# Three-pass products for gate, up and down of every expert, with a ring of four high-part buffers

## The reference, cut to what matters

```python
x = x + y                                                   # mixer's result
x = x + hier_moe(rmsnorm(x, norm_ffn[i]), w_router..., w_gate[i], w_up[i], w_down[i])

def hier_moe(h, ...):      # top 1 of 4 groups, top 2 of 4 experts in it
    hid = silu(t @ w1[e]) * (t @ w3[e]); hid = hid * gate   # w1, w3: 1024 x 512
    y = hid @ w2[e]                                         # w2: 512 x 1024
```

## Time and profile before

| | us |
|---|---|
| median of 3 runs (lowest, highest) | 1147.72 (1146.89, 1152.04) |
| span of the profiled execution | 1150.0 |
| TensorE matmul busy | 1021.1 (89%) |
| DVE busy | 621.7 (54%) |
| ACT busy | 407.2 (35%) |
| POOL busy | 135.4 (12%) |
| moved by DMA | 286.62 MB, 249 GB/s over the span |

### The profile page before, as it was taken

One profiled execution on the slowest core, in us unless ns is written; L12 is line 12 of the kernel. 1 busy time (PEld: TensorE's weight loads), 2 busy tenths in 40 slices (PEclk: granted clock), 3 DMA queues, 4 the chain that ended last, 5 costly groups with the idle time before them and its releaser, 6 DMA issues.

```text
span 1150.0 us, 13292 instructions
## 1 busy us (share of the span) xinstructions
PE 1021.1 (89%) x5002; PEld 737.4 (64%) x5002; DVE 621.7 (54%) x793; ACT 407.2 (35%) x589; POOL 135.4 (12%) x143
## 2 busy tenths in 40 slices
PE   5999997699999999997299979959999999999950
PEld 4999885356666565664199978734665656666530
DVE  5377513566565565654722384255656666565617
ACT  6225312243433434333442452214333343433403
POOL 2201200010101000010610030010010000101024
PEclk8999998799999999999599989978999999999985
DMA  8920404759999999996714031159599999999924
GB/s 249 389 75 1 167 38 166 256 181 381 355 374 361 368 350 347 378 357 251 265 49 146 17 141 49 55 175 336 201 338 372 369 358 374 353 374 350 344 84 176
DMA packets 118683, 286.62 MB, mean 249 GB/s; under 512 B 8554, under 2 KB 10090, under 8 KB 118636
## 3 DMA queue, kind: packets, MB, share of 16 engines
q1 hardware_dynamic: 104815, 236.27, 57.6%
q0 software_dynamic: 13584, 49.14, 11.4%
q10 hardware_dynamic: 244, 0.65, 0.2%
HBM read 258.06 MB, written 28.23 MB: 249 GB/s over the span
## 4 chain that ended last, share of the span: by engine, by line
PE 71%; DMA 13%; DVE 7%; issue 4%; ACT 3%; POOL 1%; SPq 1%; POOLq 0%; ACTq 0%; DVEq 0%
PE ps L621 42%; PE ps L716 14%; DMA wbuf_up<-in_w_up 10%; PE ps L724 7%; DVE x L1381 2%; PE ps L708 2%; ACT arena_c_r L1051 2%; PE ps L686 2%; PE ps L769 1%; DMA arena_a<-yrows,slots 1%; PE ps L596 1%; POOL arena_a L573 1%; DMA arena_a<-xrows,ids 1%; PE ps L740 1%; DVE arena_c L1558 1%
## 5 line engine op out<-in xcount | busy, mean ns | idle before, releaser
L716 PE MATMUL ps<-wbuf_gate,arena_a 128*128 128x512 f32 x512 | 230.5, 604 | 5.5 <-DVE arena_a L1221 5.5
L716 PEld LDWEIGHTS ps<-wbuf_gate,arena_a 128*128 128x128 f32 x512 | 98.6, 193 | 119.5 <-issue 110.6
L621 PE MATMUL ps<-wbuf_gate_r,wbuf_up_r 128*128 128x256 f32 (+1 forms) x768 | 169.5, 287 | 2.4 <-DVE wbuf_gate_r L1416 2.4
L1416 DVE TENSOR_TENSOR wbuf_down_r<-wbuf_down,arena_c_r 128x4096 fp32r<-128x4096 f32 x30 | 132.8, 4425 | 35.3 <-ACT arena_c_r L1051 35.3
L621 PE MATMUL ps<-arena_b_r,wbuf_up_r 128*128 128x264 f32 (+1 forms) x512 | 146.0, 285 | 0.0
L621 PEld LDWEIGHTS ps<-wbuf_gate_r,wbuf_up_r 128*128 128x128 f32 x768 | 129.3, 190 | 3.0 <-issue 2.7
L724 PE MATMUL ps<-wbuf_up,arena_a 128*128 128x512 f32 x256 | 117.6, 602 | 0.0
L1036 ACT ACTIVATE arena_a<-ps,vecT 128x128 f32<-128x128 f32 x128 | 36.6, 369 | 215.3 <-PE ps L708 215.3
L530 POOL DMA_INDIRECT arena_a<-xrows,ids x34 | 34.9, 1026 | 658.3 <-DVE ids L1213 657.7
L1051 ACT CAST arena_c_r<-wbuf_down 128x4096 fp32r<-128x4096 f32 x30 | 108.3, 3611 | 0.0
L1416 DVE TENSOR_TENSOR wbuf_up_r<-wbuf_up,arena_a_r 128x2048 fp32r<-128x2048 f32 x32 | 73.3, 2292 | 61.7 <-ACT arena_a_r L1058 60.1
(11 more groups left out here) (232 smaller groups left out, 1463.8 us busy)
## 6 DMA issues: line engine op xcount, KB each, us to landing
wbuf_up<-in_w_up SPq DMA_DIRECT2D x32, 2048.0 KB, 20.0
wbuf_gate<-in_w_gate SPq DMA_DIRECT2D x32, 2048.0 KB, 15.1
wbuf_down<-in_w_down SPq DMA_DIRECT2D x32, 2048.0 KB, 11.3
yrows<-arena_b POOLq DMA_DIRECT2D x32, 512.0 KB, 9.2
wbuf_gate<-in_w_in_even SPq DMA_DIRECT2D x2, 2048.0 KB, 11.0
wbuf_up<-in_w_in_even SPq DMA_DIRECT2D x2, 2048.0 KB, 9.2
wbuf_down<-in_w_out_even SPq DMA_DIRECT2D x2, 2048.0 KB, 26.2
yrows<-arena_c POOLq DMA_DIRECT2D x8, 512.0 KB, 12.3
```

Source lines behind the costliest of these rows:

```text
L621: last = pe.matmul(out, stationary[a](k), moving[b](k), start=(opens and i == 0), stop=(i == len(terms) - 1))
L716: last = pe.matmul(ps[:, 0, :], xgT[:, k, :], w[:, k, :], start=(k == 0), stop=(k == KC - 1))
L1416: dve.tensor_tensor(value_r, value, hi.bitcast(F32), ALU.subtract).then_inc(done, 1)
```

## The change

The gate and the up product become split products like the down product, and so does the last block's down product. Each matrix is handled in two groups of 2048 elements a partition. The high parts no longer have buffers of their own: four buffers of one group (`ring`) serve gate, up and down in turn, and a high part may be written when the product that used the slot last has finished its group; so `h1_mm`, `h3_mm` and `y_mm` now count groups, two a block. The low parts are still written over the loaded weights.

In body b, ACT now does: high part of group 0 of down(b-1), silu, high part of the hidden rows of b-1, group 1 of down(b-1), both groups of gate(b+1), high part of the rows of b+1 (1024 a partition out of PSUM), group 0 of up(b+1), the whole result of b-1 (1024), group 1 of up(b+1). DVE does the matching low parts, with the row numbers and the one-hot ahead of `hid`; it no longer copies results. The gate product of b waits for `xT_lo`, the low part of its rows, and for its first low group.

The norm's weight is multiplied in when the rows are scaled (`scale_rows`, odd phases), from a tile `g_ffn` that POOL loads once a layer. The final norm's weight moves to another place in SBUF.

The core of the diff:

```diff
-        up_hi = arena_a_r[:, 4608:4608 + UP_SPLIT * DE]
-        down_hi = arena_c_r[:, 0:4096]
+        ring = [arena_c_r[:, 0:GROUP], arena_c_r[:, GROUP:2 * GROUP],
+                arena_a_r[:, 6144:6144 + GROUP], arena_b_r[:, 2048:2048 + GROUP]]
...
+        def ring_slot(kind, par, g):
+            return ring[(g if par == 1 else 2 + g) if kind == GATE else
+                        (2 + g if par == 1 else g) if kind == UP else
+                        (g if par == 1 else 2 + g)]
+
+        def group_of(buf, g):
+            return buf[:, g * GROUP:(g + 1) * GROUP]
...
-                            sp.wait_ge(m[used], b - 1)
+                            sp.wait_ge(m[used], 2 * b - 2)
...
+                pool.dma_start(g_ffn, norm_ffn[l].partition_broadcast(P)).then_inc(ld_gffn, 16)
...
-                def gate(b, par, i):
-                    pe.wait_ge(ld_w[l][0][par], 16 * (before_same(b, par, i) + 1))
-                    w = as_kn(wbuf[0][par], KC)
-                    for k in range(KC):
-                        last = pe.matmul(ps[:, 0, :], xgT[:, k, :], w[:, k, :],
-                                         start=(k == 0), stop=(k == KC - 1))
-                    last.then_inc(m["h1_mm"], 1)
...
+                def first_product(kind, b, par, done):
+
+                    lo = m["gate_lo" if kind == GATE else "up_lo"]
+                    for g in range(2):
+                        pe.wait_ge(lo, 2 * b + g + 1)
+                        parts = [v.rearrange("p (c n) -> p c n", c=4)
+                                 for v in (ring_slot(kind, par, g), group_of(wbuf_r[kind][par], g))]
+                        split_product(ps[:, kind, :],
+                                      (lambda k: xT_parts[0][:, k, :], lambda k: xT_parts[1][:, k, :]),
+                                      (lambda k: parts[0][:, k - 4 * g, :], lambda k: parts[1][:, k - 4 * g, :]),
+                                      range(4 * g, 4 * g + 4), opens=(g == 0), closes=(g == 1)).then_inc(done, 1)
...
-                    pe.wait_ge(m["xT_d"], b + 1)
-                    pe.wait_ge(m["xT_a"], b + 1)
+                    pe.wait_ge(m["xT_lo"], b + 1)
...
-                down_last(2 * pairs - 1, pairs)
+                down(2 * pairs - 1, 1)
...
                 def rows_T(b):
                     need(act, m["xT_mm"], b + 1)
...
+                    act.copy(xT_flat[0], bank2(5)).then_inc(m["xT_hi"], 1)
...
+                def hi_gate(b, par, n, g):
+                    act.wait_ge(ld_w[l][GATE][par], 16 * n)
+                    need(act, m["h3_mm"], 2 * b - 1 + g)
+                    act.copy(ring_slot(GATE, par, g), group_of(wbuf[GATE][par], g)).then_inc(m["gate_hi"], 1)
+
+                def hi_up(b, par, n, g):
+                    act.wait_ge(ld_w[l][UP][par], 16 * n)
+                    need(act, m["y_mm"], 2 * b - 3 + g)
+                    act.copy(ring_slot(UP, par, g), group_of(wbuf[UP][par], g)).then_inc(m["up_hi"], 1)
+
+                def hi_down(b, par, n, g):
+                    act.wait_ge(ld_w[l][DOWN][par], 16 * n)
+                    act.wait_ge(m["h1_mm"], 2 * b + 3 + g)
+                    act.copy(ring_slot(DOWN, 1 - par, g), group_of(wbuf[DOWN][par], g)).then_inc(m["down_hi"], 1)
...
                 def body(b, par, i, last):
-                    hi_up(b, par, i)
...
+                    first = isinstance(b, int) and b == 0
+                    n = half_up(b, i)
+                    if not first:
+                        hi_down(b - 1, 1 - par, n, 0)
+                    act.wait_ge(m["h1_mm"], 2 * b + 2)
 
                     need(act, m["hid"], b)
                     act.activation(act_g, ps[:, 0, :], ACT.Silu).then_inc(m["silu"], 1)
+                    if not first:
+                        hidden_hi(b - 1)
+                        hi_down(b - 1, 1 - par, n, 1)
                     if not last:
...
+                        hi_gate(b + 1, 1 - par, n + 1, 0)
+                        hi_gate(b + 1, 1 - par, n + 1, 1)
                         rows_T(b + 1)
...
+                        hi_up(b + 1, 1 - par, n + 1, 0)
+                    if not first:
                         result(b - 1, 1 - par, (b - 1) // 2 if isinstance(b, int) else i - 1)
+                    if not last:
+                        hi_up(b + 1, 1 - par, n + 1, 1)
 
                 pairs = run_blocks(act, l, body)
+                for g in range(2):
+                    hi_down_last(2 * pairs - 1, g)
+                hidden_hi(2 * pairs - 1)
...
+                dve.scalar_tensor_tensor(out=xs[r, j, :],
+                                         in0=x[r, j, :],
+                                         scalar=rs[r, ph, j:j + 1],
+                                         in1=g_ffn[r, :],
+                                         op0=ALU.mult, op1=ALU.mult).then_inc(xs_done, 1)
...
+                dve.wait_ge(m["xT_hi"], b + 1)
+                low(xT_flat[1], bank2(5), xT_flat[0], m["xT_lo"])
...
                 def body(b, par, i, last):
                     first = isinstance(b, int) and b == 0
...
                     if not first:
...
+                        lo_group(DOWN, b - 1, 1 - par, 0)
+                        hidden_lo(b - 1)
+                        lo_group(DOWN, b - 1, 1 - par, 1)
+                    if not last:
+                        token_numbers(l, b + 2, par)
...
                     if not last:
+                        lo_group(GATE, b + 1, 1 - par, 0)
                         rows_T(l, b + 1)
...
+                        lo_group(GATE, b + 1, 1 - par, 1)
+                        lo_group(UP, b + 1, 1 - par, 0)
+                        lo_group(UP, b + 1, 1 - par, 1)
+
+                for g in range(2):
+                    lo_group(GATE, 0, 0, g)
+                for g in range(2):
+                    lo_group(UP, 0, 0, g)
                 pairs = run_blocks(dve, l, body)
```

More of the change, by code:

```diff
@@ L50 @@
 EPS = 1e-6
-UP_SPLIT = 4
+GROUP = 4 * DE
+GATE, UP, DOWN = range(3)
 MAX_OVER = 8
@@ L134, in trunk @@
         g_sgu = per_layer[:, 0:D]
+        g_ffn = per_layer[:, 0:D]
         eps = sb("eps", [P, 1])
@@ L613, in normed_tile, with split_product @@
                 transpose_tile(ph, j, (xs, x)[ph % 2][:, j, :], 4 + 2 * (j % 2)).then_inc(tr_done, 1)
-            def split_product(out, stationary, moving, chunks=range(KC), before=None, opens=True):
+            def split_product(out, stationary, moving, chunks=range(KC), before=None, opens=True, closes=True):
                 terms = [(k, a, b) for k in chunks for a, b in ((0, 0), (0, 1), (1, 0))]
@@ L735, in hidden_T, with gate, up @@
+                def gate(b, par):
+                    first_product(GATE, b, par, m["h1_mm"])
+                def up(b, par):
+                    first_product(UP, b, par, m["h3_mm"])
                 def hidden_T(b):
                     need(pe, m["hid"], b + 1)
-                    need(pe, m["hT_e"], b)
+                    need(pe, m["hT_lo"], b)
                     for c in range(FC):
@@ L743, in down @@
                 def down(b, par):
[L744 to L771, removed]
+                    need(pe, m["hT_lo"], b + 1)
@@ new lines, in down @@
+                    need(pe, m["y_out"], b)
+                    for g in range(2):
+                        need(pe, m["down_lo"], 2 * b + g + 1)
+                        parts = [v.rearrange("p (c n) -> p c n", c=2)
+                                 for v in (ring_slot(DOWN, 1 - par, g), group_of(wbuf_r[DOWN][par], g))]
+                        for k in (2 * g, 2 * g + 1):
+                            for h in range(2):
+                                cols = slice(h * 512, (h + 1) * 512)
+                                last = split_product(
+                                    ps[:, 2 + h, :],
+                                    (lambda k: hidT_parts[0][:, k, :], lambda k: hidT_parts[1][:, k, :]),
+                                    (lambda k: parts[0][:, k - 2 * g, cols], lambda k: parts[1][:, k - 2 * g, cols]),
+                                    range(k, k + 1), opens=(k == 0), closes=(k == FC - 1))
+                        last.then_inc(m["y_mm"], 1)
@@ L1030, in experts_blocks, with hidden_hi @@
                 m = moe[l]
-                row = 2 + l
                 def rows_T(b):
                     need(act, m["xT_mm"], b + 1)
-                    for c in range(4, KC):
-                        last = act.activation(xgT[:, c, :], ps[:, 6, (c - 4) * P:(c - 3) * P], ACT.Copy,
-                                              scale=vecT[:, c, row:row + 1])
-                    last.then_inc(m["xT_a"], 1)
+                    act.copy(xT_flat[0], bank2(5)).then_inc(m["xT_hi"], 1)
+                def hidden_hi(b):
+                    act.wait_ge(m["hT_mm"], b + 1)
+                    need(act, m["y_mm"], 2 * b)
+                    act.copy(hidT_flat[0], ps[:, 4, :]).then_inc(m["hT_hi"], 1)
@@ L1360, in body @@
                     if not last:
```

(19 more changed lines are left out.)

126 lines of the change are left out of this document (48 added, 78 removed).

## The result

The changed kernel takes 1195.88 us (median of 4 runs, 1191.13 to 1200.62), the kernel before beside it 1149.88. The ratio is 1.040, with a 95% interval of 1.036 to 1.043: 46 us slower, where I forecast 27. The direction was right; 1195.9 lies above the range of 1158 to 1193.

A forecast was written before the change was run, and what follows sets the result against it. TensorE was taken to bound the kernel, with DMA nearly as full. Start, bodies and end of the expert stretches gave +13.9 and +13.15 us, together +27.05 on 1150.0: 1177.1, less 2.3 for the median: 1174.8; range 1158 to 1193.

The forecast's parts named there:

- TensorE's work: Expert bodies: gate and up in three passes cut a body's work from 20.05 to 17.7 us.
- the new loop: Expert stretches: load and split before a gate product make two periods 40.7 us, one 20.35.
- E(b): End of the down product in body b, that of block b-1; the loads are issued after it.
- S(b): Start of body b's gate product; E(b) was forecast at 17.7 us after it.
- rival 3: Expert bodies: the clock falls in the idle gaps, 1 us a body, 1201, or 1188 in half of them; chance 0.16.
- S(2) to S(15): Steady part of each expert stretch, between these gate starts: +4.25 us in the first layer, +3.5 in the second.
- S(0) to S(1): First body of each expert stretch, first to second gate start: 17.9 us against 18.8, -0.9.
- S(1) to S(2): Second body of each expert stretch: 17.7 us for 20.35, -2.65.
- start and end: Each expert stretch: first gate 7.2 us later; from the last body's end to the result out, +8.0 us.
- nothing outside the stretches: Rest of the kernel outside the expert stretches: booked at 0 us.
- the norm: Row scaling with the weight: 1.7 us, some 0.9 more, ten times, hidden under other products, so 0.
- Rival 1: Expert stretches: loads come earlier and TensorE stays the bound, 1106 us; chance 0.06.

The follow-up runs named there:

- a_sp_order: The changed kernel with SP issuing each down load behind the next block's gate and up loads instead of ahead of them: 1115.09 us, ratio 0.971 to the kernel before.
- a_warm: The changed kernel with 32 extra products of 128 columns, work for nothing, behind each down product to fill the gap: 1185.38 us, ratio 1.031 to the kernel before.
- c_start: `a_sp_order` with DVE making block 0's two low gate groups ahead of the rest of `route`: 1105.09 us, ratio 0.960 to the kernel before.
- c_tail: `a_sp_order` with ACT making the last block's high down groups ahead of the result of the block before: 1100.60 us, ratio 0.955 to the kernel before.
- a_rows_first: The changed kernel with ACT copying the next rows ahead of both high gate groups, DVE following: 1168.62 us, ratio 1.017 to the kernel before.

## Why the prediction was right and wrong

**Right: TensorE's work.** Passes of 0.228 us, 17.7 us forecast for a body, 17.88 in `a_sp_order`. The gain of 2.2 us a body is real, and the changed kernel didn't collect it.

**Right: the new loop.** It runs from E(b) over load and split to the gate two bodies on; the order of the loads and the length of the way were each tested alone, with 81 and 27 us. Its cycle was forecast at 40.7 us and is 40.9 to 41.2 in the first layer, but this agreement is luck in part: two of its terms are off and nearly cancel. From S(b) to E(b) the body behind the gap takes 19.8 us and not 17.7, and the gate's load lands 15.2 us after E(b) (1.3 and 13.9) and not 16.8. The way behind it is 6.2 us, as forecast.

**Wrong in its step: every body after the first at full clock.** The sum has "TensorE idles 2.6 us a body" and then 17.7 us of work; the half clock behind the idling was left to rival 3 and stands in the sum with nothing. Since the loop spans two bodies, two interleaved chains run side by side, and only one of them waits: 3.5 us, then none. The prediction shared the wait out evenly without a reason. Behind each of the 14 longer gaps the gate ran in part at half clock. That was dear where no load's landing gives the time back: in the second body, in the last one and in the products of the mixer (below). In the loop most of it was absorbed, by what `a_warm` shows: from S(2) to S(15) the forecast is missed by only 1.6 us in the first layer and 4.8 in the second, of 22 in all.

The period of over 20 us had also seemed to be borne out by DMA, a batch needing 20.0 us from first byte to last landing. That was a time with queueing in it: at 17.88 us a body, in `a_sp_order`, the same bytes fit.

Rival 3, which I gave 0.16, named the mechanism, and its price (1188 to 1201) held the result. The price is luck in part too: its 26 us were to come from the loop, which came out 6.4 us over the forecast in both layers together. Its argument against, dense work on both sides, does not protect. The rule quoted there from the Trainium skill, TensorE: Matmul & The Clock Gate, section "HAM oscillation", fits: the clock was lower after each of these waits for a load. What stayed open in the trace of before (a 2.2 us wait to a fall, at the earlier trace rows) should have weighed more than the density.

**Mis-sized by the same cause.** S(0) to S(1) and S(1) to S(2) came out 0.5 to 2.3 us worse than forecast and the last body up to 3.1 (its gate 8.61 us at clock 0.84): in each a gate ran in part at half clock behind a gap (8.5 us for the first gate where I had 7.8; 7.35 for the second, behind a gap of 3.3 us that my own sum contains and doesn't price). Together with the last bodies this is 10.5 of the 22 us.

**Right: start and end.** +7.2 and +8.0 against +7.3 and +8.0, +7.3; `c_start` and `c_tail` name the queue order behind each.

**Wrong: nothing outside the stretches.** Of the 4.3 us between them about 3 are TensorE's: the first product of the second layer's mixer takes 4.60 us for 3.47, the products behind the mixing 23.76 for 22.43, and the mixing and the router 0.7 us more. Another 1.0 us is in two gathers (6.03 for 5.72 us, 5.67 for 4.97). Windows of the changed kernel have 0.77 there, the kernel before 1.00 at the same place:

```profile
717.00:724.00 7.00, 7.00 (x25) 5.70 (x26) 4.34 (x7) 2.78 (x4) 0.00 (x0) 0.77 0.23 82
```

```profile
693.40:700.00 6.60, 6.60 (x29) 5.36 (x30) 4.19 (x7) 2.79 (x4) 0.00 (x0) 1.00 0.24 84
```

Code and work are the same there. In `a_sp_order` the products behind the mixing take 22.43 again, but the first product 4.47. That the place of the clock's fall relative to the work decides is argued, not shown; no run was made for it, and one profile of each kernel can't tell it from chance. Why the gathers took longer stays open.

**Right with a wrong size: the norm.** 0 us; the scaling costs 1.28 us, not 1.7, and is hidden.

**Rival 1, the other side,** did not happen by itself, but the experiment that makes its condition true gave 1115 where its working gave 1106.

## What to carry to other kernels

Before an operand is put through a further stage (a split, a cast), follow its load back to the instruction that lets it be issued: a load that stands in an in-order queue behind another buffer's wait can close a loop over two iterations that had slack only while the stage was missing. A wait saved by reordering the loads was worth 81 us here, more than all arithmetic in the change. And a gap of a few microseconds in front of dense matmuls has to be priced with the half clock behind it, also where the work on both sides is dense; then ask whether the next wait absorbs that price, as the loop did here and the start and the end didn't.

## What the runs showed of the hardware that I had not expected

The busy share of the DMA engines does not say how near transfers are to their limit. It was 1.01 at 365 GB/s in the kernel before and 1.04 at 399 GB/s in `a_sp_order`: 9% more data for 3% more share, in stretches of the same loads.

Gaps of 3.4 to 4.9 us between dense products brought the clock down in every cycle of two bodies. In `a_rows_first` one of 2.8 us did so too (the gate behind it took 7.36 us); in `a_warm`, where fill products leave gaps of 0.2 to 2.2 us, the clock stayed at 1.00 from 280 to 520 us.

A gate's load took 15.3 us in `a_warm` and 14.0 in the changed kernel (medians of 12, first layer). It moved against TensorE's time, so that the cycle of two bodies stayed the same within 0.2 us.
